# A two-layer decoder trunk: attention probabilities of the two band halves added and turned as 128 columns per head

## What is computed

```
s = jnp.einsum('bnqhgd,bnkhd->bnhgqk', q, kc)        # kc: previous block and own block
diff = qi - (ku - BLK)
band = (diff >= 0) & (diff < WINDOW)                 # BLK = WINDOW = 128
mask = band[None] & (kpos >= 0)
s = jnp.where(mask[None, :, None, None], s, -jnp.inf)
mx = jnp.maximum(jnp.max(s, axis=-1, keepdims=True), sink)
p = jnp.exp(s - mx)
p = p / (jnp.sum(p, axis=-1, keepdims=True) + jnp.exp(sink - mx))
o = jnp.einsum('bnhgqk,bnkhd->bnqhgd', p.astype(vc.dtype), vc)
return o.reshape(B, S, Hq * dh) @ w_out + b_out
```

## Time and profile before

| | before |
|---|---|
| median of 3 runs | 1094.26 us (1093.18 to 1094.56) |
| the profiled execution's own time | 1094.37 us |
| its span | 1092.3 us |
| PE busy | 1084.6 us, 99% |
| DVE busy | 535.2 us, 49% |
| ACT busy | 428.9 us, 39% |
| POOL busy | 50.5 us, 5% |

### The profile page before, as it was taken

One profiled execution on the slowest core, in us unless ns is written; L12 is line 12 of the kernel. 1 busy time (PEld: TensorE's weight loads), 2 busy tenths in 40 slices (PEclk: granted clock), 3 DMA queues, 4 the chain that ended last, 5 costly groups with the idle time before them and its releaser, 6 DMA issues.

```text
span 1092.3 us, 14754 instructions
## 1 busy us (share of the span) xinstructions
PE 1084.6 (99%) x5550; PEld 909.9 (83%) x5550; DVE 535.2 (49%) x806; ACT 428.9 (39%) x748; POOL 50.5 (5%) x51
## 2 busy tenths in 40 slices
PE   9999999999999999999999999999999999999998
PEld 7888888898888888888889987789888888888886
DVE  7544578644444434333366587564343434523344
ACT  6511456543232323222355376653323232422242
POOL 1100211000000000000000024200000000000000
PEclk9999999999999999999999999999999999999999
DMA  9342327223323232122272542022323233312331
GB/s 287 106 106 79 114 84 226 74 72 86 114 78 114 78 115 77 39 96 96 96 193 59 152 100 77 1 78 83 110 85 107 87 105 90 102 35 98 97 135 77
DMA packets 141764, 109.51 MB, mean 100 GB/s; under 512 B 22480, under 2 KB 127088, under 8 KB 141728
## 3 DMA queue, kind: packets, MB, share of 16 engines
q1 hardware_dynamic: 140720, 105.84, 32.9%
q0 software_dynamic: 864, 2.92, 0.8%
q10 hardware_dynamic: 144, 0.26, 0.1%
HBM read 106.87 MB, written 2.13 MB: 100 GB/s over the span
## 4 chain that ended last, share of the span: by engine, by line
PE 96%; DVE 2%; ACT 1%; issue 0%; DMA 0%; POOL 0%; DVEq 0%; ACTq 0%; POOLq 0%
PE ps L1496 18%; PE ps L1498 18%; PE ps L1497 18%; PE ps L1744 7%; PE ps L1745 7%; PE ps L1743 7%; PE ps L1688 3%; PE ps L1690 2%; PE ps L1689 2%; PE ps L1577 1%; PE ps L1579 1%; PE ps L1578 1%; PE ps L1836 1%; PE ps L1867 1%; PE ps L1849 1%; PE ps L1643 1%
## 5 line engine op out<-in xcount | busy, mean ns | idle before, releaser
L1496 PE MATMUL ps<-act_hi,w_hi 128*128 128x512 f32 (+1 forms) x1016 | 368.8, 363 | 0.1
L1498 PE MATMUL ps<-act_hi,w_lo 128*128 128x512 f32 (+1 forms) x1016 | 366.5, 361 | 0.0
L1497 PE MATMUL ps<-act_lo,w_hi 128*128 128x512 f32 (+1 forms) x1016 | 366.5, 361 | 0.0
L1496 PEld LDWEIGHTS ps<-act_hi,w_hi 128*128 128x128 f32 x1016 | 191.7, 189 | 31.1 <-DVE w_lo L927 0.9
L1498 PEld LDWEIGHTS ps<-act_hi,w_lo 128*128 128x128 f32 x1016 | 191.8, 189 | 29.1
L1497 PEld LDWEIGHTS ps<-act_lo,w_hi 128*128 128x128 f32 x1016 | 191.8, 189 | 29.1 <-issue 0.2
L1745 PE MATMUL ps<-w_hi,w_lo 128*128 128x512 f32 x288 | 112.1, 389 | 0.0
L1743 PE MATMUL ps<-w_hi 128*128 128x512 f32 x288 | 112.1, 389 | 0.0
L1744 PE MATMUL ps<-w_lo,w_hi 128*128 128x512 f32 x288 | 112.1, 389 | 0.0
L753 ACT ACTIVATE arena<-ps,vecs 128x512 f32<-128x512 f32 x44 | 34.3, 779 | 188.6 <-PE ps L1498 188.6
L1262 DVE SCALAR_TENSOR_TENSOR arena<-ps,vecs,arena 128x511 f32<-128x511 f32 x44 | 33.0, 749 | 144.4 <-ACT arena L753 144.4
(11 more groups left out here) (208 smaller groups left out, 1218.6 us busy)
## 6 DMA issues: line engine op xcount, KB each, us to landing
raw<-in_f_w_up SPq DMA_DIRECT2D x88, 512.0 KB, 4.6
raw<-in_f_w_down SPq DMA_DIRECT2D x44, 512.0 KB, 3.3
raw<-in_m_w_in SPq DMA_DIRECT2D x23, 512.0 KB, 4.1
raw<-in_m_w_out SPq DMA_DIRECT2D x8, 512.0 KB, 3.3
raw<-in_a_w_in SPq DMA_DIRECT2D x16, 256.0 KB, 4.5
raw<-in_a_w_out SPq DMA_DIRECT2D x16, 256.0 KB, 4.8
h<-in_x SPq DMA_DIRECT2D x4, 512.0 KB, 7.5
h<-in_x_turned SPq DMA_DIRECT2D x3, 512.0 KB, 6.9
```

The lines of the kernel that those rows point to most:

```text
L1496: nc.tensor.matmul(dst, uh[:, k], zh, start=(k == 0), stop=False)
L1497: nc.tensor.matmul(dst, uh[:, k], zl, start=False, stop=False)
L1498: ins = nc.tensor.matmul(dst, ul[:, k], zh, start=False, stop=(k == KT - 1))
```

## The change

- POOL adds the two halves of a step's probabilities before it multiplies them (`fold`), so that 128 columns per head are left, and PE turns 4 blocks per step and not 8, each step into a bank of its own (2 or 3).
- ACT copies the turned block to the first half of `p_t` (outside block 0). POOL multiplies that in place by a 0/1 mask of k > q (`keep_prev`), and DVE writes the second half from PSUM, masked by k <= q (`keep_own`). `mix` and the next scores of an even step wait for these in place of the copies.
- PE turns both steps of a pair one after the other, and the `turn` of a normed block goes to the end of the pair.
- ACT's exponentials of the next even step go ahead of the two copies. The high parts of output units 4 and 5 move from pair 2 to pair 1, those of 6 and 7 to the head of pair 2.
- DVE does the low parts of units 4 and 5 in pair 1 with `inverse(4)` ahead of them, and 6 and 7 at the end of pair 2. Each `inverse(2m+2)` moves ahead of the norms.

The diff, cut to its core:

```diff
+        prev_keys = arena[:, 46 * KB + P:46 * KB + 2 * P]
...
-            for s in range(AT_STEPS):
-
-                b, lo = s % 4, P if s < ASTEPS else 0
+            nc.gpsimd.memset(prev_keys, 1.0).then_inc(pool_done, 1)
+            pool.wait_ge(pool_done, 10)
+            nc.gpsimd.affine_select(out=prev_keys, in_=prev_keys, compare_op=ALU.is_gt, fill=0.0, base=0,
+                                    pattern=[[-1, P]], channel_multiplier=1).then_inc(pool_done, 1)
...
+            def fold(s):
+
+                b = s % 4
                 pool.wait_ge(inv_done, s + 1)
-                nc.gpsimd.tensor_tensor(sc[:, b, :, lo:], sc[:, b, :, lo:],
-                                        asm[:, b, 5].unsqueeze(2).to_broadcast([P, AG, 2 * P - lo]),
+                own = sc[:, b, :, P:]
+                if s >= ASTEPS:
+                    nc.gpsimd.tensor_tensor(own, own, sc[:, b, :, 0:P], ALU.add).then_inc(pf_done, 1)
+                    pool.wait_ge(pf_done, s - ASTEPS + 1)
+                nc.gpsimd.tensor_tensor(own, own, asm[:, b, 5].unsqueeze(2).to_broadcast([P, AG, P]),
                                         ALU.mult).then_inc(pn_done, 1)
+
+            def keep_prev(s):
+
+                pool.wait_ge(pt_done, s + 1)
+                part = p_t[:, s % 2, :, 0:P]
+                nc.gpsimd.tensor_tensor(part, part, prev_keys.unsqueeze(1).to_broadcast([P, AG, P]),
+                                        ALU.mult).then_inc(prev_done, 1)
+
+            for m in range(A_PAIRS):
+                for s in (2 * m, 2 * m + 1):
+                    fold(s)
+                if 2 * m >= ASTEPS:
+                    for s in (2 * m, 2 * m + 1):
+                        keep_prev(s)
...
-                b, blk = s % 2, s // ASTEPS
+                part = slice(P, 2 * P) if s < ASTEPS else slice(0, P)
                 act.wait_ge(pt_mm, s + 1)
...
+                nc.scalar.copy(p_t[:, s % 2, :, part], ps[:, 2 + s % 2].rearrange("p (j k) -> p j k", j=AG))\
+                    .then_inc(pt_done, 1)
...
+                if m + 1 < A_PAIRS:
+                    probs(2 * m + 2)
                 for s in (2 * m, 2 * m + 1):
                     turned(s)
...
+                if m + 1 < A_PAIRS:
+                    probs(2 * m + 3)
...
+            def keep_own(s):
+
+                dve.wait_ge(pt_done, s + 1)
+                nc.vector.scalar_tensor_tensor(p_t[:, s % 2, :, P:], causal[:].unsqueeze(1).to_broadcast([P, AG, P]),
+                                               0.0, ps[:, 2 + s % 2].rearrange("p (j k) -> p j k", j=AG),
+                                               ALU.is_equal, ALU.mult).then_inc(own_done, 1)
...
+                if 2 * m >= ASTEPS:
+                    for s in (2 * m, 2 * m + 1):
+                        keep_own(s)
+                if m + 1 < A_PAIRS and m != 1:
+                    inverse(2 * m + 2)
                 for w in pair_work(m, "post") + pair_work(m, "pre"):
                     work(w)
-                if m + 1 < A_PAIRS:
-                    inverse(2 * m + 2)
+                if m == 2:
+                    for k in range(6, KT):
+                        split_lo(G_AOUT + k)
...
+                elif s >= 2 * ASTEPS:
+                    pe.wait_ge(own_done, s - 2 - ASTEPS)
                 elif s >= 3:
                     pe.wait_ge(pt_done, s - 2)
...
-                if s % 2:
-                    pe.wait_ge(pt_done, s)
-                elif s + 2 < AT_STEPS:
+                if s % 2 == 0 and s + 2 < AT_STEPS:
                     pe.wait_ge(mx_done, s + 3)
                 for j in range(AG):
...
+                    ins = nc.tensor.transpose(ps[:, 2 + s % 2, j * P:(j + 1) * P], sc[:, b, j, P:], ident[:])
...
-                pe.wait_ge(pt_done, 2 * m + 2)
+                if blk == 0:
+                    pe.wait_ge(pt_done, 2 * m + 2)
+                else:
+                    pe.wait_ge(own_done, 2 * m + 2 - ASTEPS)
+                    pe.wait_ge(prev_done, 2 * m + 2 - ASTEPS)
...
                 turn_probs(2 * m)
+                turn_probs(2 * m + 1)
                 filling(m, 2)
-                turn_probs(2 * m + 1)
+                filling(m, 3)
                 for w in pair_work(m, "turn"):
                     work(w)
-                filling(m, 3)
```

More of the change, by code:

```diff
@@ L258, in trunk @@
         pn_done = sem("pn_done")
+        pf_done, own_done, prev_done = sem("pf_done"), sem("own_done"), sem("prev_done")
         qb_mm = sem("qb_mm")
@@ L538, in _ @@
                                     ALU.subtract).then_inc(w_lo_done, 1)
-            for s in range(AT_STEPS):
-                b, lo = s % 4, P if s < ASTEPS else 0
-                pool.wait_ge(inv_done, s + 1)
-                nc.gpsimd.tensor_tensor(sc[:, b, :, lo:], sc[:, b, :, lo:],
-                                        asm[:, b, 5].unsqueeze(2).to_broadcast([P, AG, 2 * P - lo]),
-                                        ALU.mult).then_inc(pn_done, 1)
+            nc.gpsimd.memset(prev_keys, 1.0).then_inc(pool_done, 1)
+            pool.wait_ge(pool_done, 10)
+            nc.gpsimd.affine_select(out=prev_keys, in_=prev_keys, compare_op=ALU.is_gt, fill=0.0, base=0,
+                                    pattern=[[-1, P]], channel_multiplier=1).then_inc(pool_done, 1)
+            pool.wait_ge(pool_done, 11)
+            def fold(s):
+                b = s % 4
+                pool.wait_ge(inv_done, s + 1)
+                own = sc[:, b, :, P:]
[3 more added lines that the diff above has]
+                nc.gpsimd.tensor_tensor(own, own, asm[:, b, 5].unsqueeze(2).to_broadcast([P, AG, P]),
+                                        ALU.mult).then_inc(pn_done, 1)
+            def keep_prev(s):
[9 more added lines that the diff above has]
+                        keep_prev(s)
         @block.scalar
@@ L842, in turned @@
             def turned(s):
-                b, blk = s % 2, s // ASTEPS
+                part = slice(P, 2 * P) if s < ASTEPS else slice(0, P)
                 act.wait_ge(pt_mm, s + 1)
-                lo = P if blk == 0 else 0
-                nc.scalar.copy(p_t[:, b, :, lo:], ps[:, 2:4].rearrange("p a (j k) -> p (a j) k", k=2 * P)
-                               [:, :, lo:]).then_inc(pt_done, 1)
+                nc.scalar.copy(p_t[:, s % 2, :, part], ps[:, 2 + s % 2].rearrange("p (j k) -> p j k", j=AG))\
+                    .then_inc(pt_done, 1)
             def mixed_hi(m):
@@ L882, in _ @@
                 if m == 2:
-                    for k in range(4, 6):
+                    for k in range(6, KT):
                         split_hi(G_AOUT + k)
@@ L886, in _ @@
                     mixed_hi(m - 1)
-                if m == 2:
-                    for k in range(6, KT):
-                        split_hi(G_AOUT + k)
+                if m + 1 < A_PAIRS:
+                    probs(2 * m + 2)
                 for s in (2 * m, 2 * m + 1):
                     turned(s)
[L892 to L895, removed]
+                if m == 0:
+                    split_hi(G_AOUT + 3)
+                if m == 1:
+                    for k in range(4, 6):
+                        split_hi(G_AOUT + k)
+                if m + 1 < A_PAIRS:
+                    probs(2 * m + 3)
             for w in pair_work(A_PAIRS - 1, "turn"):
@@ L1461, in _ @@
                 if m == 1:
[L1462 to L1465, removed]
+                    add_a_bias(8, 1, S // 2, S)
+                    inverse(4)
+                    for k in range(4, 6):
                         split_lo(G_AOUT + k)
+                    add_a_bias(9, 1, S // 2, S)
+                if 2 * m >= ASTEPS:
[3 more added lines that the diff above has]
+                    inverse(2 * m + 2)
                 for w in pair_work(m, "post") + pair_work(m, "pre"):
                     work(w)
-                if m + 1 < A_PAIRS:
-                    inverse(2 * m + 2)
+                if m == 2:
+                    for k in range(6, KT):
+                        split_lo(G_AOUT + k)
             for w in pair_work(A_PAIRS - 1, "turn"):
```

## The result

| | before | changed, first timing | changed, second timing |
|---|---|---|---|
| median of all executions, us | 1093.88 | 1098.24 | 1096.78 |
| median without the two disturbed, us | 1093.88 | 1096.90 | 1096.78 |
| lowest to highest of these, us | 1093.18 to 1094.56 | 1096.02 to 1099.00 | 1096.47 to 1100.32 |
| ratio to before, 95% interval | 1 | 1.0031 [1.0021, 1.0041] | 1.0034 [1.0020, 1.0048] |

A forecast was written before the change was run, and what follows sets the result against it. PE's own work was taken as the bound; 6.2 us gained and 6.2 given back in stalls left 1094.37 for the profiled execution, median 1094.3. The forecast's own range was 1092.1 to 1096.7, the wider range 1090.0 to 1097.4.

The forecast's parts named there:

- The gain, 6.2: PE's own work across the attention: 6.2 us less, from halved transposes and fewer changes from transposes to projections.
- The 5.3 of the halved transposes: PE's probability transposes: four in place of eight take 0.44 us less for each of 12 steps, 5.3 us.
- The 0.9 for a saved change from transposes to projections: PE, both steps turned together: one change less in each of 8 pairs, at 0.11 us each, 0.9 us.
- The stalls, 6.2: New waits of PE at five places, summed to 6.2 us given back, with ends of 4.0 to 8.5.
- A: `turn(0,0)` at pair 5's end: PE waits for `inverse(12)` behind POOL, then a norm; 2.0 us taken, up to 2.75.
- B: `turn_probs(15)`: PE waits for POOL's add and multiply behind DVE's inverses and norm halves; 1.9 us taken, 0 to 2.4.
- D: `turn(1,0)` at pair 7's end: the norm `pre` waits for POOL's mask multiply of step 15; 0.5 us taken.
- E: First slice of `out(3)`, behind the last turn: PE waits for the bias of line 950; 0.9 us.
- C: `turn_probs(7)`: PE waits for POOL's adds and multiplies behind two inverses and two splits; 0.9 us, ends 0 and 1.8.
- The first rival: Faster: POOL's and DVE's instructions slip past each other, stalls only 1.7 us, 4.5 gained; 1089.8 us, chance 0.22.
- The second: Slower rival: POOL and DVE's two-operand work add up and bound the pairs, transposes give nothing; 1097.6 us, chance 0.20.
- The rest: What no row shows, such as a lower granted clock once PE has waits; no time given, chance 0.03.

## Why the prediction was right and wrong

I said no change that can be told (0.53) and 1094.3 us; it is slower by 0.3%, which had 0.22. The range, 1090.0 to 1097.4, holds the second timing (1096.78) and not the first as the median of all nine executions (1098.24; 1096.90 over seven). The shape was right: transposes that gain, and single waits at turns, transposes and the first `out(3)` slice that give it back. What was wrong in the sum, taken together, went to one side.

- **The gain, 6.2.** It is 5.2: 0.87 for each of pairs 2 to 7, as pair 4 shows, which has no wait. The 5.3 of the halved transposes held. The 0.9 for a saved change from transposes to projections did not, for the longer set took back what the change gave: both steps turned together take 673.51 - 672.72 = 0.79 (the time of the eight transposes in the earlier trace rows), more than twice the 0.35 of the earlier trace rows, and pairs 0 and 1, which lost a change and nothing else, kept their 7.17 and 9.74.
- **The stalls, 6.2.** They are 6.97 as the profile counts them. A: 2.45 (I took 2.0, with an upper end of 2.75). ACT's copies came later, POOL starting 2.6 us after the turn and not 1.3, because the exponentials ahead of them (line 863 below, the copies 871) waited for the maxima, the reason that I gave for that end; and the norm waited out a mask. B: 1.29 (1.9), inside its ends. D: 0.35 (0.5). E: 0.75 (0.9). That the sum came near 6.2 is in part luck: B was 0.6 too long, and C, next, too short for a reason that I had wrong.

```profile
683.62 0.51 ACT L863 ACTIVATE arena<-arena 128x256 f32<-128x256 f32 x1 [1.53 <-DVE arena L1420]
...
685.70 1.05 ACT L871 COPY arena<-ps 128x512 f32<-128x512 f32 x2
```

- **C, 0.9, named the wrong waiter.** I let POOL's `fold` of step 7 hold up the second set of transposes. The wait of 1.69 is at the first set, `turn_probs(6)`, which also waits for the masked maximum of step 8 because their bank is the same. On DVE `inverse(7)` stands ahead of `masked_max(8)`, and the splits ahead of both. I had the two splits back to back in 2.35 from the earlier trace rows; they took 4.37, each blocked by a POOL instruction. There POOL's one instruction ended 0.3 us behind both, and I read from it that DVE keeps its place between two of its own instructions. In B I had let POOL's add go between two halves of a norm, so my sum used both readings. In the attention DVE did not keep its place, with POOL waiting; why that row differs stays open. The same mechanism in pair 4 (norm halves of 2.19 and 2.17) makes the 0.44 at step 10, which I had not priced at all.
- **A wait costs PE more than the idle time that the profile shows.** Of pairs 2 to 7 and the end, 6.97 of waits less 5.2 gained gives 1.8, and 2.8 is lost. The 1.0 between them stands at the six waits. The profile counts idle time from the end that it shows for the last projection (687.16 + 0.39), but a `turn` that waits for nothing starts 0.23 after that projection's start (700.71 to 700.94). So at 690.00 the loss is 690.00 - 687.16 - 0.23 = 2.61 and not 2.45. The same count gives some 0.16 at four of the waits, 0.2 at the one between two sets of transposes and 0.07 at the end, 0.9 in all. The rest is that work behind a wait takes a little longer: the waiting `turn` takes 0.59 to the next instruction, the one that did not wait 0.53.

Start to start, as my sum had counted them, the stalls are then 8.0 and not 6.2. With 1.0 less of gain that makes the 2.8 us that the sum lacks.

Point by point of what else I had said: where nothing blocks it, POOL's add takes 1.27 to 1.30 and its mask 1.26 to 1.29 (1.27 taken), the multiply 1.04 (1.02), `keep_own` 0.69 (0.75). The estimate of 1.12 for the add, from 4497 ns for 2048 elements on the Trainium skill's page "GPSIMD Engine Reference", section 3.1, was too low; here the measured 1.28 decides, and the nearest row was the better source. The mask's building was hidden, ACT's copies added to a wait of PE at A alone of the places that I had named, and the scores and mixes of the changed kernel never waited for the masks.

The first rival (POOL and DVE slip past each other, 1089.8) fell: the norms took 1.82 to 2.19, and 1.23 to 1.27 in the earlier trace rows. The second (POOL and two-operand DVE work as the bound of every pair, 1097.6) came nearest to the measured time, but for another reason: pairs 2, 4 and 6 are as short as PE's work. Something like it, with PE waiting for POOL in nearly every pair, came only when POOL got 2.54 us more, and then at the mix and not ahead of the transposes. The rest, a lower granted clock once PE has waits, had 0.03 and no price. As far as the mean clocks tell, it is what sets the four longer executions of the changed kernel apart; none of them was profiled, so this is not shown.

## What to carry to other kernels

When GpSimd gets work beside VectorE, count for each VectorE instruction with two SBUF operands that meets waiting GpSimd work one GpSimd instruction more, and ask which instruction is next in line on each side when the other engine's ends: moving two short instructions was worth 3.2 us here, taking GpSimd's masks away in the old order 1.8. Where an instruction waits for several semaphores, follow every one back through the other engines' lists, above all the one that only frees a bank. On a saturated PE a gain in its own work is safe only with all its suppliers re-timed for the shorter pair; with the masks made on DVE from PSUM, the inverses ahead and the turns behind the next mix, it became 4.8 us faster than the kernel before in place of 3 us slower.

## What the hardware showed that I had not expected

**Turns, instruction by instruction.** In the places of the attention read here no engine kept its place between two of its own instructions while the other waited: the norm of 1.28 went between two masks that stand next to each other on POOL (3.57 for the pair of them), and POOL's add went between two splits (4.37). It is not shown as a rule: in the earlier trace rows POOL's 256-element operation stood beside two splits that went back to back, and it does the same in the changed kernel (2.85 us).

**The granted clock falls after some waits of PE.** In the profiled execution of the kernel with the masks from PSUM (columns as in the earlier trace rows, the clock third from the end):

```profile
685.00:690.00 5.00, 2.61 (x12) 1.80 (x10) 4.93 (x13) 2.90 (x14) 1.14 (x1) 0.96 0.00 0
690.00:695.00 5.00, 4.99 (x22) 3.50 (x24) 1.45 (x4) 2.13 (x5) 4.39 (x4) 0.50 0.00 2
```

PE was busy 2.61 of 5 us, with its wait of 2.4 at the end, and then worked 5 us at the lower level (0.50, which is 1.2 GHz). This execution took 1098.43, and the median of that kernel is 1094.98. The profiled executions of the changed kernel (a wait of 2.45 at the same place) and of the kernel with the turn before the filling (3.8) kept the full clock there. So a wait of 2.4 us on PE was paid twice in one execution, and waits of 2.45 and 3.8 us in two others were not; the runs do not show what decides it. None of the 10 executions of the kernel with the masks from PSUM and the inverse first, where the longest wait is 0.7, is above 1092.0.
